# Output tail of a one-layer decoder step: eight of sixteen tiles stored early and completed by accumulating transfers

## What is computed

```python
def ffn_block(x, shift, scale, gate, g_pre, w1, w2, g_post):
    h = rms_norm(x, g_pre) * (1.0 + scale) + shift
    f = jnp.square(jax.nn.relu(h @ w1)) @ w2
    return x + gate * rms_norm(f, g_post)
```

## Time and profile before

| what | value |
|---|---|
| median of 3 runs | 1468.25 us (1466.19 to 1468.3) |
| profiled execution | 1466.55 us, of which its span (first to last instruction) 1464.9 us |
| PE busy | 1432.4 us, 98% of the span |
| DVE, ACT, POOL busy | 814.8, 524.9, 116.2 us |
| DMA moved | 319.06 MB, mean 218 GB/s |

### The profile page before, as it was taken

The page is one execution under the profiler, slowest core; times in us unless marked ns, Lnnn a source line. Parts: engine busy times, 40 slices in busy tenths (PEclk is TensorE's granted clock), DMA queues, the critical chain, the costliest instruction groups (busy, mean ns, idle before and its releaser), DMA issues.

```text
span 1464.9 us, 26870 instructions
## 1 busy us (share of the span) xinstructions
PE 1432.4 (98%) x10278; PEld 1315.3 (90%) x10278; DVE 814.8 (56%) x1317; ACT 524.9 (36%) x753; POOL 116.2 (8%) x195
## 2 busy tenths in 40 slices
PE   6999999999999999999999999999999999999996
PEld 2788877888788879999999999999999999999996
DVE  5677668757655678674434554443554334555554
ACT  4333244443435654333223333322333323333331
POOL 1111000275210000000000000000000000000002
PEclk9999999999999999999999999999999999999998
DMA  9999888887799777444446445446444444444431
GB/s 377 347 339 333 340 304 307 296 295 275 283 356 348 279 281 289 149 153 157 149 166 231 144 147 168 144 144 247 154 145 152 155 152 144 144 143 146 156 99 72
DMA packets 88459, 319.06 MB, mean 218 GB/s; under 512 B 12240, under 2 KB 12496, under 8 KB 87744
## 3 DMA queue, kind: packets, MB, share of 16 engines
q1 hardware_dynamic: 79776, 290.49, 55.9%
q0 software_dynamic: 5360, 25.14, 4.6%
q10 hardware_dynamic: 3248, 2.39, 0.5%
HBM read 312.18 MB, written 5.80 MB: 217 GB/s over the span
## 4 chain that ended last, share of the span: by engine, by line
PE 92%; DVE 3%; DMA 2%; ACT 1%; issue 1%; POOL 1%; SPq 0%; POOLq 0%; ACTq 0%; DVEq 0%
PE bank L1580 73%; PE bank L1633 8%; PE bank L1556 3%; PE bank L1540 2%; DMA raw<-in_stream 2%; PE bank L1905 2%; PE bank L1820 1%; DVE w_lo L813 1%; PE bank L1751 1%; PE bank L1780 1%; PE bank L1763 0%; ACT w_hi L418 0%; PE bank L1850 0%; PE bank L1567 0%; PE bank L1706 0%
## 5 line engine op out<-in xcount | busy, mean ns | idle before, releaser
L418 ACT ACTIVATE w_hi<-raw 128x1024 fp32r<-128x1024 f32 x352 | 361.6, 1053 | 271.5 <-PE bank L1580 232.0
L813 DVE TENSOR_TENSOR w_lo<-raw,w_hi 128x1024 fp32r<-128x1024 f32 x352 | 419.5, 1225 | 41.6 <-ACT w_hi L418 40.0
L1580 PE MATMUL bank<-m_hi,w_hi 128*128 128x320 f32 x1280 | 397.2, 310 | 0.0
L1580 PE MATMUL bank<-m_hi,w_lo 128*128 128x320 f32 x1280 | 395.5, 309 | 0.0
L1580 PE MATMUL bank<-m_lo,w_hi 128*128 128x320 f32 x1280 | 395.5, 309 | 0.0
L1580 PE MATMUL bank<-h_hi,w_hi 128*128 128x320 f32 x1216 | 378.7, 311 | 0.0
L1580 PE MATMUL bank<-h_hi,w_lo 128*128 128x320 f32 x1216 | 375.7, 309 | 0.0
L1580 PE MATMUL bank<-h_lo,w_hi 128*128 128x320 f32 x1216 | 375.7, 309 | 0.0
L1580 PEld LDWEIGHTS bank<-m_hi,w_hi 128*128 128x128 f32 x1280 | 240.2, 188 | 12.0 <-issue 12.0
L1580 PEld LDWEIGHTS bank<-h_hi,w_hi 128*128 128x128 f32 x1216 | 228.2, 188 | 13.9 <-issue 13.8
L1580 PEld LDWEIGHTS bank<-m_lo,w_hi 128*128 128x128 f32 x1280 | 240.3, 188 | 0.0
(11 more groups left out here) (241 smaller groups left out, 1127.9 us busy)
## 6 DMA issues: line engine op xcount, KB each, us to landing
raw<-in_stream SPq DMA_DIRECT2D x544, 512.0 KB, 4.6
k_pages<-in_kc POOLq DMA_DIRECT2D x16, 512.0 KB, 7.3
v_pages<-in_vc POOLq DMA_DIRECT2D x16, 512.0 KB, 5.2
x<-in_x_cm SPq DMA_DIRECT2D x4, 640.0 KB, 6.7
x_mid<-in_x_cm POOLq DMA_DIRECT2D x1, 2560.0 KB, 10.5
x<-in_x_cm POOLq DMA_DIRECT2D x1, 2560.0 KB, 14.0
v_out<-v_cm POOLq DMA_DIRECT2D x1, 1280.0 KB, 8.8
k_out<-back POOLq DMA_DIRECT2D x1, 1280.0 KB, 5.5
```

What stands on the lines that cost most here:

```text
L418: act.activation(w_hi[2 * (j % 2) + h][:, :], raw[slot][:, h * 1024:(h + 1) * 1024], ACT.Copy).then_inc(hi_ready, 1)
L813: dve.tensor_tensor(w_lo[q][:, :], raw[slot][:, h * 1024:(h + 1) * 1024], w_hi[q][:, :], ALU.subtract).then_inc(half_used[slot][h], 1)
L1580: last = pe.matmul(bank[j % 2][:, 0:T], w[q][:, k * P:(k + 1) * P], v[:, 8 * h + k, :], start=(h == 0 and k == 0 and n == 0), stop=(h == 1 ...
```

## The change

It stores the eight tiles 0 to 7 of `x`, as they stand after `residual`, to `y_out` during the MLP: one transfer of POOL's queue, issued when `x_home` and `residual_added` have come, and waited for by POOL. At the end, DVE multiplies these eight tiles of `back` by `RSTD3` in place, four at a time, and POOL issues two transfers (`add_out`) that add them onto what `y_out` holds, one ahead of each of its own two entries of the table. The other eight tiles go the old way, DVE with 8 to 12 and POOL with 13 to 15, and SP stores them in four transfers. POOL waits for its two at its end.

```diff
-PIECES = [("dve", 0, 4), ("pool", 11, 13), ("dve", 4, 8), ("pool", 13, 15), ("dve", 8, 11), ("pool", 15, KT)]
+PIECES = [("pool", 13, 15), ("dve", 8, 11), ("dve", 11, 13), ("pool", 15, KT)]
+ADDED = [(0, 4), (4, 8)]
...
         dve.wait_ge(prompt_gated, KT)
         dve.wait_ge(rstd3_wide, 1)
         turn = 0
+        for first, end in ADDED:
+            dve.tensor_tensor(back[:, first:end, :], back[:, first:end, :], wide(RSTD3, end - first), ALU.mult).then_inc(
+                y_scaled, 1)
         for name, first, end in PIECES:
             if name == "dve":
                 parts = PARTS[:, 0:end - first, :]
...
         pool.dma_start(x[:, :, :], x_cm).then_inc(x_home, 16)
 
         pool.wait_ge(x_home, 16)
+        pool.wait_ge(residual_added, 12)
+        pool.dma_start(y_out[:, 0:ADDED[-1][1], :], x[:, 0:ADDED[-1][1], :]).then_inc(x_kept, 16)
+        pool.wait_ge(x_kept, 16)
+
+        def add_out(n):
+            first, end = ADDED[n]
+            pool.wait_ge(y_scaled, n + 1)
+            pool.dma_start(y_out[:, first:end, :], back[:, first:end, :], accum_op=ALU.add).then_inc(y_added, 16)
+
         pool.wait_ge(prompt_gated, KT)
         pool.wait_ge(rstd3_copied, 1)
-        for name, first, end in PIECES:
-            if name == "pool":
-                part = back[:, first:end, :]
-                mine.then(pool.tensor_tensor(part, part, rstd[:, :].unsqueeze(1).to_broadcast([P, end - first, T]), ALU.mult))
-                pool.tensor_tensor(x[:, first:end, :], x[:, first:end, :], part, ALU.add).then_inc(x_pool, 1)
+        for n, (first, end) in enumerate([(f, e) for name, f, e in PIECES if name == "pool"]):
+            add_out(n)
+            part = back[:, first:end, :]
+            mine.then(pool.tensor_tensor(part, part, rstd[:, :].unsqueeze(1).to_broadcast([P, end - first, T]), ALU.mult))
+            pool.tensor_tensor(x[:, first:end, :], x[:, first:end, :], part, ALU.add).then_inc(x_pool, 1)
+        pool.wait_ge(y_added, 16 * len(ADDED))
```

More of the change, by code:

```diff
@@ L269, in decoder_step @@
     x_dve, x_pool = S("x_dve"), S("x_pool")
-    y_stored = S("y_stored")
+    y_stored, x_kept, y_scaled, y_added = S("y_stored"), S("x_kept"), S("y_scaled"), S("y_added")
     def use_of(use, off):
```

## The result

The changed kernel has a median of 1473.47 us (1472.17 to 1474.88, 6 runs) beside 1468.52 us of before in the same jobs: a ratio of 1.0036, 95% interval 1.0026 to 1.0046. It is slower, by 3.8 to 6.8 us. The forecast of +1.7 (1469.9), within noise, was too low by 3 us; the range to 1475.5 held the result.

The account below looks back on a forecast made before the run. The tail was taken as bound by elementwise work, with the DMA engines close behind. Accumulations at f = 1.94 move the data end from 1463.3 to 1465.0, early store free: 1468.25 + 1.7 = 1469.9 us, range 1466.5 to 1475.5.

Parts of the forecast that it names:

- The price of the accumulation: Tail, DMA engines: each 640 KB accumulation costs a load plus a store, 3.27 us, against 1.68 for a plain store.
- The span ends 1.1 us behind: End of kernel: the last piece lands at 1463.8 and the span ends 1.1 us behind that.
- POOL's issue: Tail, POOL: each issue occupies it for 0.55 us; its last tile is ready at 1459.8, 1.6 less than before.
- the last rival: Tail, POOL: an accumulating issue costs 1.5 us instead of 0.55, making POOL the bound, +0.3 to +1; chance within others, 0.03.
- DVE: Tail, DVE: its work ends at 1459.25 instead of 1460.64, 1.4 us less.
- the early store, free: MLP: the 1280 KB store hides in the weight stream and costs nothing, at most 3.4 us without that cover.
- no gain even at f = 1: Tail, DMA engines: with accumulations as cheap as plain stores, the end stays at 1463.3, no change.
- the DMA engines as the second bound: Tail: behind the elementwise work the DMA engines are a close second bound, ending at 1463.3 before the change.
- Each 0.1 of f above 1.4 adds 0.34: Tail, DMA engines: how the predicted loss grows with the accumulation's price, in us.
- the prediction's own pause: Tail, DMA engines: at f = 1 they idle from 1456.8 to 1458.3, before the first plain store can start.
- The rival of a slow accumulation: Tail, accumulating transfers: few packets in flight, 6 us each with two rows at a time, +4 to +7; chance 0.30.
- the forecast's own case: Tail: f between 1.5 and 2.3, +0.3 to +2.9 us, likeliest 1468.5 to 1471.2; chance 0.47.

Follow-up runs that it names:

- the floor of 10.0: The changed kernel with SP storing the first eight tiles plain, without x, and POOL issuing and waiting for nothing in the tail: ratio 0.9979 to before, tail 10.0 us.
- POOL only issues: The changed kernel with POOL's tiles given to DVE, POOL only issuing both accumulations, and SP waiting for them: ratio 1.0018 to before, tail 15.0 us.

## Why the prediction came out as it did

**The price of the accumulation** was taken too low: f, in plain stores of 1.68 us for each 640 KB, was put at 1.94. The share of the 16 engines that each queue's packets took, over 17 us of the tail (1453 to 1470), is of the changed kernel, and then of the kernel with plain transfers on POOL's queue and SP waiting:

```profile
q0 software_dynamic: 288, 1.31, 47.8%
q1 hardware_dynamic: 576, 1.31, 20.2%
```

```profile
q1 hardware_dynamic: 576, 1.31, 20.3%
q0 software_dynamic: 288, 1.31, 19.2%
```

1.31 MB accumulated take 8.1 us of the engines: f = 8.1 / 3.36 = 2.4. Plain by the same queue they take 3.3. The run with a single accumulation of four tiles gives 2.4 as well (4.0 / 1.68). Two parts of this are seen apart in half a us each of the changed kernel, the first from 1456.5 and the second from 1459.5 (packets, MB, share). A packet's whole time is counted to the window it begins in, or a share couldn't pass 100%:

```profile
q0 software_dynamic: 16, 0.08, 195.1%
```

```profile
q0 software_dynamic: 20, 0.10, 101.0%
```

In the steady part a packet takes 1.01 x 0.5 x 16 / 20 = 0.40 us. A plain one of the same bytes takes 0.20 (40 packets at 98.9% in the run with plain transfers). That is 2.0, and the estimate from a load and a store, 1.94, was right for it. The Trainium skill, "Collectives: The Full Stack", section "The bandwidth ceiling: the fold count and why AG ≠ RS ≠ AR", says that a reducing transfer is slow because of its second source; the trace agrees in the steady part, 0.40 beside 0.20, though no run here shows the second read itself. But the first packet of each engine takes 1.95 x 0.5 x 16 / 16 = 0.98 us, and for about 2 us the engines give half of even the slow rate (110 beside 209 GB/s). The prediction had no term for that. It isn't POOL's queue: the first packets of the plain transfer on it take 0.20 each, seen in half a us from 1456.5 of the run with SP waiting:

```profile
q0 software_dynamic: 7, 0.04, 17.6%
```

Why the start of an accumulation is slow was only seen, not taken apart.

**What ends the kernel** was read wrongly. "The span ends 1.1 us behind" SP's last landing took the 1.1 for a constant. Of it, 0.7 was POOL's drain, which ended at 1464.6 where SP was through at 1463.9; the prediction had no term for the drain. The changed kernel's wait at POOL's end put the drain behind the last accumulation: the data end at 1468.3 or so and the span 3.2 later, against 1.6 before. Before with POOL waiting last shows it alone: +2.4 in the trace, 1.0022 in time.

**POOL's issue.** Predicted 0.55 and no more. In the trace, from DVE's end of the first multiplication (1454.6) to the next multiplication's end (1457.7) it is 3.1, against 1.53 + 0.55 predicted: 0.6 ahead of the issue, 0.91 for it, and a first instruction behind it of 1.88 that overlaps it. POOL's last tile was ready 8.84 us into the tail, not 7.6 as forecast. So the last rival, an issue of 1.5 instead of 0.55, has the right size for the first issue (3.1 - 1.53 = 1.6) though the instruction itself took 0.91; the second cost about 0.9 (from 1459.31 to 1461.02, less 0.86). Its outcome didn't come: POOL's last tile was ready 0.4 earlier than before (8.84 instead of 9.23 into the tail), not 0.3 later, and POOL wasn't the bound.

**Right were**: DVE (its last addition ends 6.86 into the tail, forecast 7.06); the early store, free (0.9995, and PE busy for 10.00 of 10 us in the changed kernel where it goes out, 655 to 665); no gain even at f = 1 by way of POOL's queue (1.0001); the bytes per us at half with the share full, 209 GB/s at 1.03; and the DMA engines as the second bound right behind the elementwise work.

**The sum again**, in tails: forecast +1.7. The data end 15.2 into the tail where 12.8 was forecast: +2.4, of which 1.6 is f (8.1 - 6.5), 0.7 the later start of the data (1456.7, which is 3.6 into the tail, instead of 2.9), and 0.1 unassigned. POOL's wait and drain: +1.6 (3.2 instead of 1.6 behind the data). Together 5.7, as measured. By experiments, from the floor of 10.0: POOL's queue instead of SP's +2.9 (12.9; of it 0.9 the later start of the data, 1.5 the pause), accumulating instead of plain +3.4 (16.3), POOL's wait +2.1 (18.4). In the timing the first two steps stand clear (0.9979, 1.0001, 1.0033); the third lies within the intervals there, and is shown in time only on the kernel before.

**A slip in the sum.** "Each 0.1 of f above 1.4 adds 0.34" leaves out the prediction's own pause: up to f = 1.9 the first accumulation is over before the first plain store can start (1458.3), so only the second one counts, 0.17 for each 0.1 from f = 1 on. At f = 1.5 that is +0.9, not +0.3. The forecast at 1.94 isn't touched.

**The rival of a slow accumulation** had the right size (+4 to +7) by a mechanism that the traces don't bear out. With a round trip of 1.5 us and one or two rows at a time, an engine would end a packet every 1.5 or 0.75 us; after the start it ends one every 0.40. The accumulations did land 6.2 and 8.4 us behind their issue, but beside full DMA engines, not idle ones. The upper edge of the range, 1475.5, came from this rival: the forecast's own case ended at 1471.2. That the range held the result is in part luck.

No version with the addition beat the kernel before. The one that was faster, plain on SP's queue, leaves the addition out.

## What to carry to other kernels

Before moving an addition into the store, see whether the DMA engines have room: here they were the second bound, and an accumulated byte took 2.4 times the engine time of a plain one, of which a slow start of some 2 us per transfer is part; plain stores of another queue stood behind it. No run here shows a case in which it paid. Look which engine's closing drain ends the span before touching the tail: here a wait at GpSimd's end, for its own transfers or others', put some 3 us behind the last landing, and the same wait on SyncE some 0.3, or what is left of the 1.7 behind GpSimd's own last transfer. Price a transfer that no row shows by its start and its steady rate apart, and widen the range by the start.

## What the runs showed of the hardware that was not expected

GpSimd's drain ends about 3.2 us behind its last instruction (1461.42 to 1464.6) or takes 3.2 to 3.4 behind its last wait; if it has to hold for a transfer of its own queue, it ends 1.7 to 1.8 behind that one's landing (four runs with SP waiting: two accumulations, one of eight tiles, plain, POOL only issues). SyncE's takes 7 ns.

The start of an accumulating transfer slows the engines for other queues too: at 1461.5 to 1462.5 of the changed kernel 113 GB/s in all, though of SP's first two stores, 0.82 MB and issued from 1459.34 on, only 0.29 MB had moved by 1461.5. When the second accumulation followed directly on the first (POOL only issues), the share of POOL's queue was 43.5% of the same 17 us, instead of 47.8% in the changed kernel and 46.5% with SP waiting; with a single transfer of eight tiles it was 42.4%. That would fit a start that costs less when the engines are already accumulating; with one profile each and plain stores mixed in, it isn't shown.
